# Second attention of a two-layer decoder step: weights folded into differences of V's rows

## The reference, cut to what matters

```python
z = jnp.einsum('bqhd,bkhd->bhqk', qb, kb).astype(jnp.float32) * scale
q_pos = q_pos0 + jnp.arange(start, stop)
mask = jnp.arange(k_end)[None, :] < q_pos[:, None]
log_1m = jnp.where(mask, jax.nn.log_sigmoid(-z), 0.0)
suffix = lax.cumsum(log_1m, axis=3, reverse=True) - log_1m
a = jnp.where(mask, jnp.exp(jax.nn.log_sigmoid(z) + suffix), 0.0)
outs.append(jnp.einsum('bhqk,bkhd->bqhd', a.astype(v.dtype), vb))
```

## Time and profile before

| what | value |
|---|---|
| median of 3 runs | 1648.67 us (1648.11 to 1648.92) |
| profiled execution, span | 1647.5 us |
| what a run's time has beside such a span | about 1.2 us |
| PE busy, share of the span | 98% |
| DVE busy | 70% |
| ACT busy | 45% |
| "vs" and the start of "qb" on PE | up to 938.4 us, from 938.4 us |
| second attention on PE | from about 998 us to 1158.2 us |

### The profile page before, as it was taken

One profiled execution on the slowest core, in us unless ns is written; L12 is line 12 of the kernel. 1 busy time (PEld: TensorE's weight loads), 2 busy tenths in 40 slices (PEclk: granted clock), 3 DMA queues, 4 the chain that ended last, 5 costly groups with the idle time before them and its releaser, 6 DMA issues.

```text
span 1647.5 us, 31458 instructions
## 1 busy us (share of the span) xinstructions
PE 1616.3 (98%) x13140; PEld 1483.3 (90%) x13140; DVE 1151.9 (70%) x1605; ACT 740.6 (45%) x1228; POOL 145.7 (9%) x123
## 2 busy tenths in 40 slices
PE   8999999999999999999999999999999999999999
PEld 6888766699999999999999896666999999999999
DVE  5765477668984797488742328989689848974874
ACT  5444366765541344134432215768555413531441
POOL 0000000012210011012000000000122201110110
PEclk9999999999999999999999999999999999999999
DMA  7133899941222122222244358996412221221222
GB/s 286 52 111 132 350 418 418 419 160 52 86 94 103 52 78 103 77 78 78 103 166 140 112 209 360 420 418 288 167 66 89 95 85 52 103 102 53 78 103 90
DMA packets 39596, 265.45 MB, mean 161 GB/s; under 512 B 4256, under 2 KB 4640, under 8 KB 10272
## 3 DMA queue, kind: packets, MB, share of 16 engines
q1 hardware_dynamic: 36720, 252.95, 39.8%
q0 software_dynamic: 2736, 10.49, 1.8%
HBM read 247.69 MB, written 15.73 MB: 160 GB/s over the span
## 4 chain that ended last, share of the span: by engine, by line
PE 85%; DVE 8%; DMA 3%; issue 2%; ACT 2%; SPq 0%; DVEq 0%; ACTq 0%
PE ps L584 30%; PE ps L799 28%; PE ps L268 5%; PE ps L269 4%; PE ps L270 4%; PE ps L1260 2%; PE ps L1319 2%; DVE s_lo L748 2%; PE ps L611 2%; PE ps L1204 2%; DMA kv<-in_v_a 1%; PE ps L1238 1%; DMA xT<-in_v_a 1%; PE ps L1225 1%; DVE pw L1621 1%
## 5 line engine op out<-in xcount | busy, mean ns | idle before, releaser
L230 ACT ACTIVATE w_hi<-w_raw 128x2048 fp32r<-128x2048 f32 x55 | 105.1, 1910 | 190.3 <-PE ps L584 158.5
L246 DVE TENSOR_TENSOR w_lo<-w_raw,w_hi 128x2048 fp32r<-128x2048 f32 x55 | 126.0, 2291 | 71.4 <-ACT w_hi L230 71.4
L744 ACT ACTIVATE s_hi<-t 128x512 fp32r<-128x512 f32 x176 | 109.4, 626 | 144.6 <-PE ps L799 65.8
L799 PE MATMUL ps<-hs_hi,s_hi 128*128 128x320 f32 x528 | 163.8, 310 | 0.0
L799 PE MATMUL ps<-hs_hi,s_lo 128*128 128x320 f32 x528 | 163.2, 309 | 0.0
L799 PE MATMUL ps<-hs_lo,s_hi 128*128 128x320 f32 x528 | 163.1, 309 | 0.0
L584 PE MATMUL ps<-gu_hi,w_hi 128*128 128x320 f32 x692 | 157.9, 309 | 0.2
L584 PE MATMUL ps<-gu_lo,w_hi 128*128 128x320 f32 x692 | 157.7, 309 | 0.0
L584 PE MATMUL ps<-gu_hi,w_lo 128*128 128x320 f32 x692 | 157.6, 309 | 0.0
L748 DVE TENSOR_TENSOR s_lo<-t,s_hi 128x512 fp32r<-128x512 f32 x176 | 132.8, 760 | 5.4 <-ACT s_hi L744 4.6
L268 PE MATMUL ps<-w_hi,h_hi 128*128 128x512 f32 x320 | 126.8, 396 | 8.1 <-DVE h_lo L300 8.1
(11 more groups left out here) (298 smaller groups left out, 3995.9 us busy)
## 6 DMA issues: line engine op xcount, KB each, us to landing
w_raw<-in_w SPq DMA_DIRECT2D x99, 1024.0 KB, 4.8
kv<-in_k_a SPq DMA_DIRECT2D x12, 1024.0 KB, 16.1
kv<-in_v_a SPq DMA_DIRECT2D x12, 1024.0 KB, 16.7
kv<-in_v_s SPq DMA_DIRECT2D x12, 1024.0 KB, 12.6
kv<-in_k_s SPq DMA_DIRECT2D x12, 1024.0 KB, 15.0
xT<-in_k_a SPq DMA_DIRECT2D x8, 1024.0 KB, 17.4
xT<-in_k_s SPq DMA_DIRECT2D x8, 1024.0 KB, 11.7
work<-in_v_a SPq DMA_DIRECT2D x7, 1024.0 KB, 14.9
```

Source lines behind the costliest of these rows:

```text
L230: nc.scalar.activation(w_hi[s][:, :, :], w_raw[:, s, :, :], ACT.Copy).then_inc(hi_done, 1)
L246: nc.vector.tensor_tensor(w_lo[s][:, :, :], w_raw[:, s, :, :], w_hi[s][:, :, :].bitcast(F32), ALU.subtract).then_inc(lo_done, 1)
L744: nc.scalar.activation(s_hi[i][:, :, :], factor(j % 2, i), ACT.Copy).then_inc(hi_done, 1)
L799: last = nc.tensor.matmul(ps[:, bank[i], 0:HALF], w[:, p, :], m[:, p, :], start=(i < 3 and p == 0 and a == 0), stop=(p == 3 and a == 2), s ...
```

## The change: what it does, and the diff

- The prompt steps of the second attention lose `act_px` and the multiplication in `dve_prod`. What the scan leaves in `odds(k, n)` (the suffix products S) is transposed as it is.
- The copies out of PSUM compute 1 - S: `act_pt` with scale -1 and bias 1, `dve_pt` as a two-operation `tensor_scalar`.
- Four buffers (`self.left`) take turns where two did; `act_pu(k)` waits for the transposes of step k-4. `pe_ps` waits for `pu`.
- V's prompt rows in `v5` become differences to the row before, in four column quarters: a DMA copies a quarter shifted down by one row into `shift` (the memory of `swt0`), rows 0 to 126 to partitions 1 to 127, and the last partition of each tile to partition 0 of the next; DVE then subtracts in place. `shift` is one buffer, so the copy of quarter q waits for the subtraction of q-1, which also waits until V's half has been stored to HBM.
- V's store is split in two halves. All of these DMAs are on POOL's queue.
- On DVE the subtractions stand ahead of `h_lo` tiles 0 and 4, and at the heads of "qb" units 2 and 3. `pe_pv` waits for the quarter that it reads.

```diff
@@ pe_pt, pe_pv, pe_ps
-                self.wait(pe, s["pz" if self.b else "px"], k)
+                self.wait(pe, s["pu" if self.b else "px"], k)
...
-                    src = (self.pp if self.b else self.pw)[k % 2][:, c, j * P:(j + 1) * P]
+                    src = self.odds(k, (k % QB + 1) * P)[:, c, j * P:(j + 1) * P] if self.b else \
+                        self.pw[k % 2][:, c, j * P:(j + 1) * P]
...
                 if i == 0:
                     self.wait(pe, s["po"], t)
+                    if self.b:
+                        pe.wait_ge(kq["diff"], t // 2 + 1)
@@ act_pu, odds, act_pt, dve_pt, dve_prod
-                self.wait(act, s["pw"], k - 1)
+                if k > 3:
+                    act.wait_ge(s["pt"], self.rounds(k - 3))
...
-                return self.pw[k % 2][:, :, SEQ - n:SEQ]
+                return self.left[k % 4][:, :, SEQ - n:SEQ]
...
-                                     ps[:, self.pt_bank(k, r), 0:n * P], ACT.Copy).then_inc(s["pe"], 1)
+                                     ps[:, self.pt_bank(k, r), 0:n * P], ACT.Copy, bias=1.0 if self.b else 0.0,
+                                     scale=-1.0 if self.b else 1.0).then_inc(s["pe"], 1)
...
-                nc.vector.tensor_copy(wt[:, k % 2, 0:n, :].rearrange("p b q -> p (b q)"),
-                                      ps[:, self.pt_bank(k, 0), 0:n * P]).then_inc(s["pd"], 1)
+                nc.vector.tensor_scalar(wt[:, k % 2, 0:n, :].rearrange("p b q -> p (b q)"),
+                                        ps[:, self.pt_bank(k, 0), 0:n * P], -1.0, 1.0, ALU.mult, ALU.add)\
+                    .then_inc(s["pd"], 1)
...
                     last = nc.vector.tensor_tensor_scan(y, y, y, 1.0, ALU.mult, ALU.min)
-                ch.link(last)
+                last.then_inc(s["pw"], 1)
                 if between is not None:
                     between()
-                nc.vector.wait_ge(s["pz"], k + 1)
-                x = self.pp[p][:, :, 0:n]
-                nc.vector.tensor_tensor(x, x, self.pw[p][:, :, SEQ - n + 1:SEQ + 1], ALU.mult).then_inc(s["pw"], 1)
@@ new functions
+        shift = swt0[:, :].rearrange("p (t c) -> p t c", t=QB)
+        def v_quarter(q, rows, tiles):
+            return v5[rows, tiles, q * UC:(q + 1) * UC]
+        def shift_v(pool, q):
+            pool.wait_ge(kq["vev"], (1 + q // 2) * TT)
+            if q > 0:
+                pool.wait_ge(kq["diff"], q)
+            nc.gpsimd.dma_start(shift[1:P, :, :], v_quarter(q, slice(0, P - 1), slice(0, QB))).then_inc(kq["shifted"], 16)
+            nc.gpsimd.dma_start(shift[0:1, 1:QB, :], v_quarter(q, slice(P - 1, P), slice(0, QB - 1)))\
+                .then_inc(kq["shifted"], 16)
+        def diff_v(dve, ch, q):
+            if q == 0:
+                ch.link(nc.vector.memset(shift[0:1, 0:1, :], 0.0))
+            dve.wait_ge(kq["shifted"], 32 * (q + 1))
+            dve.wait_ge(kq["stored"], 48 + q // 2 * 16)
+            v = v_quarter(q, slice(0, P), slice(0, QB))
+            nc.vector.tensor_tensor(v, v, shift[:, :, :], ALU.subtract).then_inc(kq["diff"], 1)
@@ POOL's stream
-            pool.wait_ge(kq["vev"], 2 * TT)
-            nc.gpsimd.dma_start(o_vs.rearrange("(t p) c -> p t c", p=P), v5[:, :, :]).then_inc(kq["stored"], 16)
+            for q in range(4):
+                if q % 2 == 0:
+                    pool.wait_ge(kq["vev"], (1 + q // 2) * TT)
+                    half = slice(q // 2 * 2 * UC, (q // 2 + 1) * 2 * UC)
+                    nc.gpsimd.dma_start(o_vs[:, half].rearrange("(t p) c -> p t c", p=P), v5[:, :, half])\
+                        .then_inc(kq["stored"], 16)
+                shift_v(pool, q)
@@ DVE's stream
             for t in range(KT):
+                if t in (0, 4):
+                    diff_v(dve, ch, t // 4)
                 dve.wait_ge(mix1["hi"], t + 1)
...
+            def b_begin(j):
+                if j in (2, 3):
+                    diff_v(dve, ch, j)
+                if j == 3:
+                    tb.dve_b_begin(dve, ch)
```

More of the change, by code:

```diff
@@ L1098, in __init__ @@
                 self.s = sems("t" + layer, "kused vused "
-                              "ps px pw pt pe pv po q s x w0 w1 w2 wev wn wne pvs oev otr o hi his lo los" +
-                              (" pu pz u p pd" if self.b else " pm nm rl sq sh sl ms ln rstd y"))
+                              "ps pw pt pe pv po q s x w0 w1 w2 wev wn wne pvs oev otr o hi his lo los" +
+                              (" pu u p pd" if self.b else " px pm nm rl sq sh sl ms ln rstd y"))
                 self.s.update(landing)
@@ L1103, in __init__ @@
                 self.pp = (pp0, pp1 if self.b else pp1_a)
+                self.left = (pp0, pw0, pp1, pw1)
                 self.pw = (pw0, pw1 if self.b else pw1_a)
@@ L1252, in pe_s @@
                 if n == 0:
-                    pe.wait_ge(s["pz" if self.b else "px"], 1)
+                    pe.wait_ge(s["pu" if self.b else "px"], 1)
                 for h in part:
@@ L1414, in act_px @@
                 act, s, p, n = nc.scalar, self.s, k % 2, (k % QB + 1) * P
[L1415 to L1427, removed]
+                act.wait_ge(s["pm"], k + 1)
+                self.wait(act, s["pw"], k - 1)
+                for c in range(2):
+                    last = nc.scalar.activation(self.pp[p][:, c, 0:n], ps[:, B_PS + c, 0:n], ACT.Exp,
+                                                bias=st[:, 8 + 2 * p + c:9 + 2 * p + c], scale=-1.0,
+                                                accum_out=st[:, 12 + 2 * p + c:13 + 2 * p + c])
+                last.then_inc(s["px"], 1)
             def odds(self, k, n):
-                return self.pw[k % 2][:, :, SEQ - n:SEQ]
+                return self.left[k % 4][:, :, SEQ - n:SEQ]
             def act_pt(self, k, r):
@@ L1551, in act_b @@
                 self.act_pu(0)
-                self.act_px(0)
                 self.act_sx(0)
@@ L1560, in act_b @@
                     self.act_pu(k + 1)
-                    self.act_px(k + 1)
                     if n % 2 == 0:
@@ L1571, in act_b @@
                         self.act_pu(k + 2)
-                        self.act_px(k + 2)
                     if n >= N_PAIRS - 5:
@@ L1615, in dve_prod @@
             def dve_prod(self, ch, k, between=None):
-                s, p, n = self.s, k % 2, (k % QB + 1) * P
+                s, n = self.s, (k % QB + 1) * P
                 nc.vector.wait_ge(s["pu"], k + 1)
@@ L1764, in dve_b_begin @@
             def dve_b_begin(self, dve, ch):
-                nc.vector.memset(pw0[:, :, SEQ:SEQ + 4], 1.0)
                 nc.vector.memset(sw[:, KEYS:KEYS + 4], 1.0)
@@ L1779, in dve_b @@
                 dve.wait_ge(kq["qev"], KT)
-                nc.vector.memset(pw1[:, :, SEQ:SEQ + 4], 1.0)
                 self.dve_q(0, slice(KT // 2, KT))
@@ L1873, in sub_y @@
                     .then_inc(s["y"], 1)
-        kq = sems("b", "kev vev qev stored")
+        kq = sems("b", "kev vev qev stored shifted diff")
         mix1 = sems("mix1", "hi lo free")
@@ L1893, in kq_dve @@
             for j in range(4):
-                if j == 3 and ahead is not None:
-                    ahead()
+                if ahead is not None:
+                    ahead(j)
                 if j < 3 or not last:
@@ L2083, in _ @@
             nc.scalar.preload_act_table_set("sigmoid_and_others")
-            tb.act_b(act, "ob", [(kq["stored"], 48)])
+            tb.act_b(act, "ob", [(kq["stored"], 64)])
             nc.scalar.preload_act_table_set("natural_log_exp_and_others")
@@ L2148, in _ @@
                     .then_inc(mix1["lo"], 1)
-            kq_dve(dve, "qb", kq["qev"], 0, SCALE, True, lambda: tb.dve_b_begin(dve, ch),
+            def b_begin(j):
[3 more added lines that the diff above has]
+                    tb.dve_b_begin(dve, ch)
+            kq_dve(dve, "qb", kq["qev"], 0, SCALE, True, b_begin,
                    between=lambda: tb.dve_sprod(ch, 0))
-            tb.dve_b(dve, ch, "ob", [(kq["stored"], 48)])
+            tb.dve_b(dve, ch, "ob", [(kq["stored"], 64)])
             residual_dve(dve, "ob", lambda e: first_los(e, "g10", range(4)), pair_dve(norms["ffn1"]), x_back=48)
```

## The result

The kernel with the change took 1738.03 us (median of 5 runs, 1737.84 to 1740.32), beside 1648.11 us for the kernel before: ratio 1.0557, 95% interval 1.0545 to 1.0569, 90 us slower. The forecast was 1645.9 us with a range to 1652.0 us. The profiled execution has a span of 1736.2 us against 1647.5 us.

The account below looks back on a forecast made before the run. PE was taken to bound the kernel, so only its waits on DVE and ACT count: 1.95 + 0.6 + 0.2 = 2.75 us, other parts costing nothing. 1648.67 - 2.75 = 1645.9 us, range 1641.8 to 1652 us.

Parts of the forecast that it names:

- What bounds the kernel: Whole span: PE, busy 98% at full clock, sets the time, so a gain exists only where PE waits.
- The subtractions: DVE before and in "qb": four of 1.23 us, 4.9 us in all; quarter 1's copy takes 6.6 us, no cost.
- the shadow: Start of "qb": subtraction 1 done by 938.4, tile 4 ready at 939.3, PE wants it at 941.91; slack 2.6 us.
- Rival 2: V's shifted copies: 127 partitions miss some of 16 DMA engines, 22.5 us per copy on one, 1671 us; chance 0.15.
- the exception: Shifted copies: the skill page's note that some direct GpSimd copies were seen on all 16 engines, eight partitions each.
- The waits that go: Attention stage: PE's waits for late `sp_b` 1.95 us, for ACT's copies 0.6 and 0.2, sum 2.75 us saved.
- rival 4: Attention stage: more falls away, two "issue" stretches (2.6 us) as well, giving 1643.3 us; chance 0.10.
- "issue" stretches: Attention stage: five PE idle stretches up to 1.4 us, some 6.5 us in sum, ended by neither DVE nor ACT; expected to stay.
- Rival 1: Attention stage: gain eaten on PE's own stream by longer "issue" waits, gain 0 to 1.3 us, 1648.0 us; chance 0.20.
- Rival 3: Start of "qb": copy spread but late, quarter 1 lands at 944.7, PE stands 4.9 us, 1650.8 us; chance 0.05.
- The copies that compute 1 - S: ACT's and DVE's copies out of PSUM in the attention stage: scale and bias add nothing.
- The loads as a limit: Attention stage: K and V loads are saturated, so PE can gain 6 to 7 us before it waits for them.

Follow-up runs that it names:

- e9: e1 with a DVE tensor_tensor of the removed multiplication's shape put back ahead of the transposes; 1647.25 us, ratio to the kernel before 1.0001.
- e5: The change with only the 127-partition copies, without the small 3 KB copy; 1738.51 us (one run).
- e1: The change with each 127-partition copy issued as two, of 112 and 15 partitions (spread version); 1642.80 us, ratio to the kernel before 0.9972.
- e3: The change's attention steps alone, V left as it is: no shifted copies, subtractions or waits for them; 1643.42 us, ratio to the kernel before 0.9973.
- e8: e1 with quarter 3 copied as 127 partitions, quarters 0 to 2 still as 112 and 15; 1670.90 us (one run).
- e10: e1 with ACT's first activation of each prompt step done twice, restoring ACT's removed load; 1643.38 us, ratio to the kernel before 0.9980.
- e11: e1 with both DVE's multiplication and ACT's second activation put back; 1652.67 us, ratio to the kernel before 1.0033.
- e7: e1 with each shifted copy issued as 96 and 31 partitions instead of 112 and 15; 1647.16 us (one run).
- e2: The change with copies of all 128 partitions to the same partitions, no shift, no small copy; 1643.75 us (one run).

## Why the prediction was wrong, point by point

- **What bounds the kernel: right.** PE sets the end wherever it has no gap, and putting DVE's work back lengthens the stage again (e9).
- **The subtractions: the step that failed.** "With a 1 MB weight load beside it I take 6.6 us", for a copy of 127 partitions, by a row of a 128-partition store. The unspread copy takes 35.9 us (e5). Spread, it does what was said: landed before 935.1 where 937.2 was forecast, cost nothing (e1, e3). The place in the queue and the shadow were right, the number of engines was not: spread copies land in 5.4 to 5.9 us (e1), and 127 partitions had one engine.
- **Rival 2 was the right mechanism with a chance of 0.15, and its price was under a third of the true one** (25 against the 87 us of waits). Three terms were too small or missing. The copy: 22.5 us against 35.9 us. Copy 1 of e5 has the DMA queues to itself and takes 32.8 us: 5.2 us until its first packet (the issue on POOL alone takes 4.6 us), then 8 us in which only 23 of its 127 large packets move beside the 1905 small ones, then 19 us at 23 GB/s. Copies beside loads took up to 45.0 us, and POOL stands 5.3 us before one that is issued behind the store. The chain: each copy starts only after the subtraction before it, so I counted quarters 1 and 3, while all four stopped PE (19.0, 29.6, 12.6, 26.2 us). The clock: 6 to 7 us of restarts, which I had not counted at all. e8 shows the same for quarter 3 alone: 27 to 28 us, of which I had 4.
- **The rule on the number of engines.** The section "Why a DMA increments its semaphore by 16 and not by 1" of *DMA: Bandwidth & Descriptors* in the Trainium skill says that the engine count is the largest up to 16 that divides the slowest dimension: 127 gives one engine. The runs agree (by the share and the packets one engine for 127 and 31, by the packets 14 for 126, 15 for 15 and 16 for 128, 112 and 96). It also says that some direct copies from GpSimd were seen on all 16 with 127 partitions; this one was not. With a chance of 0.15 for rival 2 I had let the exception decide; the rule held.
- **The waits that go: right in place, low in size.** 2.75 us were summed; the stage lost 5.3 us in e1 and the run 4.6 us by the ratio, 5.1 us by the medians. The late `sp_b` (2.5 us in five places) is gone from e1's view, one wait for `sp` of 0.3 us came up early in the stage. Of ACT's waits the two at L1225 went, and the other two stayed at 1.1 us in sum, where I had taken 0.2 us off. With the copies spread the kernel would have landed at rival 4's 1643.3 us, but by luck and not by its mechanism. In PE's rows the waits for DVE and ACT fell from 2.9 to 1.4 us and the "issue" stretches from 6.5 to 5.0 us; the other 2.3 us of the stage are too short for a record and stay open. One kind of wait the prediction overlooked, that of the weight loads for `swn`, in the kernel before and in e1:

```profile
PEld ps L1269 <- DVE swn L1668: 5.3, 7, 0.8
```

```profile
PEld ps L1273 <- DVE swn L1663: 3.7, 7, 0.6
```

It is back at 5.2 us in e9, but it is 7.2 us in the fast e10, so it can't be priced from these rows.

- **Rival 1 (the gain is eaten) did not happen**, and its "issue" stretches are not tied to the gain: e1 has five, as the kernel before, two of them down to 0.4 us, and their sum is 5.0 us in e1, 6.7 in e3, 4.3 in e9 and 2.1 in e10. The traces point at what ends them. All 25 that are over 0.3 us, in the six kernels with a trace of this stage (before, e1, e3, e9, e10, e11), end 2.4 to 2.7 us after a packet of 16 KB starts on the queue that the page's part 3 calls "instruction"; such packets come every 5 to 10 us, and PE's waits for DVE and ACT end anywhere from 0.4 to 8.6 us behind one. That fits a PE that stands until its next instructions have come. No run varied it.
- **Smaller things.** Rival 3 adds 13.2 to 930.6 and has 944.7; it is 943.8, so tile 4 is ready at 945.9, PE stands 4.0 us and the time is 1649.9 us. It changes no chance. DVE is busy 15.9 to 16.2 of 21 us in e1, where 15.5 was to show.
- **The copies that compute 1 - S: right.** `dve_pt` takes 690 ns (692 before), ACT's 512-column copy 602 ns with scale and bias (611 before).
- **The loads as a limit: right.** DMA share stays at 1.01 in the stage, and the first short wait of PE for V (0.3 us) shows up in e10.

## What to carry to other kernels

Before a DMA is put on a path, look at the largest divisor up to 16 of its partition count: 127 and 31 have none but 1 and ran on one engine, and cutting 127 into 112 and 15 turned a loss of 90 us into a gain of about 5 beside the median of the kernel before. A trace shows it at once as a DMA share of 0.06. When two engines and the DMA queue are within 5% of each other, put a removed instruction back by itself to see whose time it was; here DVE's 26 us were worth 3 to 4.5 us, ACT's 23 us next to nothing as long as DVE's were gone. Look at the granted clock of such a run before the whole difference is put down to the instruction: of e9's 4.3 us it made 1.7.

## What the runs showed of the hardware that had not been expected

- A 508 KB copy with 127 partitions ran on one DMA engine, 23 GB/s, from POOL's queue and from ACT's alike; with 128 or 126 partitions it landed in 5.8 us. 31 partitions ran on one engine too (e7).
- On POOL the unspread copy is also dearer to issue (4.6 us against 0.8 us for 128 partitions in e2), and 1905 packets of 16 bytes go with its 127 packets of 4 KB. The number of such packets fits the engine count: 465 for 31 partitions, 18 for 126, 1 for 15, none for 96, 112 and 128.
- PE's granted clock fell to 0.50 (1.2 GHz) in each gap of the change and stayed there for the first 3 to 4 us of work; four gaps cost 6 to 7 us on top of their own length. Waits of 1.87 us (e7), 2.1 us (e9) and 1.7 us (e11) were each followed by a stretch at 0.50 that cost 1.7 us of work; a wait of 2.1 us in e3 was not.
- Stretches of 0.3 to 2.1 us in which PE waits for nothing that the profile names end 2.4 to 2.7 us after a 16 KB packet starts on the instruction queue, 25 times of 25.
